# A hybrid decoder block: the short convolution with sequence rows on partitions, its shifted copies made by DMA; first loads and last scalings in another order

## The chip, the core and the metric

The kernel runs on one core of a Trainium2 chip. The core has TensorE (PE, with its weight loads as PEld), VectorE (DVE), ScalarE (ACT), GpSimd (POOL) and SyncE (SP), which work from queues of their own and meet at semaphores, and 16 DMA engines that serve the DMA queues of SyncE and of ScalarE. The metric is the device time of one execution in microseconds (us).

## What is computed

The reference, cut to what matters. All of it is float32; x is 1 x 256 x 2048.

```python
proj = rmsnorm(x, norm_mix) @ w_in          # q, k, v, o, i, f, cb, cc, cx, ga, gb
hm = mlstm_chunkwise(q, k, v, i + b_igate, f + b_fgate)     # 8 heads, chunks of 128
y_a = (sigmoid(o) * rmsnorm_per_head(hm) * mh_norm) @ w_branch_a
p = cc * cx                                  # 256 rows x 2048 channels
u[t] = conv_w[0]*p[t-2] + conv_w[1]*p[t-1] + conv_w[2]*p[t]   # zero ahead of row 0
y_b = (cb * u) @ w_branch_b
x = x + (sigmoid(ga) * y_a + sigmoid(gb) * y_b) @ w_out
x = x + (silu(hf @ w_gate) * (hf @ w_up)) @ w_down          # hf = rmsnorm(x, norm_ffn)
out = rmsnorm(x, norm_final)
```

## The kernel before

**Products.** A float32 product is made of three in `float32r`: the activations and the weights are each split into a rounded part (`_hi`) and a rest (`_lo`), and hi*hi, hi*lo and lo*hi are summed in PSUM. The weights come in chunks of 1 MB (128 partitions x 2048 columns). SyncE loads a chunk into one of four `w_raw` slots, ScalarE rounds it into `w_hi` (`split`, through `copy` at L616), VectorE subtracts into `w_lo` (`split`, L1064), TensorE multiplies: 16 products of 512 columns with `w_hi`, then 8 with `w_lo`. `w_hi` and `w_lo` have two slots. A slot of `w_raw` is free once `w_lo` is made (`lo_split`), one of `w_lo` once TensorE has ended the chunk (`lo_used`). Every engine runs an order written out by hand and waits on counting semaphores.

**Stages.** The head (x and its norm; the chunks of q and k; the gates), three pairs of column blocks for q, k and v, then four turns of the convolution, then six pairs (`p` = FRONT = 3 to 8; o, ga, gb), then the two branches (`G_Y`), the output projection, the feed-forward and the final norm. In pairs, steps named in `FRONT_S` (4 and 6 in pair FRONT) save a product by sums of weights: there VectorE makes sums (`front_sums`, L1165 to L1170), and `t_lo` (L1193).

**A turn of the convolution** (`conv_turn(i)`, a block of 512 channels) has 12 chunks, j = 0 to 11: cb, cc, cx. The results leave with sequence rows on partitions, 2 x 128 rows: ScalarE takes cb into `nat` (j = 3), TensorE transposes it (`turn_block`, j = 5), ScalarE copies it into `cbT`. Later `nat` takes cc (j = 7), and VectorE multiplies it by cx at the turn's end (L1367, `dve_out`). In the next turn TensorE transposes that too (`turn_p`, behind j = 0), and ScalarE copies it (`p_taken`) into `pT`, which has room for zeros ahead of row 0, and scaled by the last tap into `uT`. With channels on partitions a shift in time is a shift of columns, and a tap is one number per partition: VectorE adds the two other taps (`conv_0` at j = 0, `conv_1` at j = 1, four operations of 256 columns each), multiplies by `cbT`, and after ScalarE's `cu_high` makes `cuT_lo` (`conv_low`, j = 2). The turns also carry two heads of the mLSTM each (`head_turn` behind j = 2, `head_scores` behind j = 3, `head_first`, `head_second` behind j = 6 to 9). The last block's taps fall into pair FRONT, in its steps j = 0, 1, 2. Turns 1 to 3 are a hardware loop (`Fori`) on each engine.

**Head.** SyncE issues `norm_mix`, the first quarter of x, three small loads, and then the first chunk in two halves (L437). TensorE warms up on transposes of `ident`, transposes `vec_rows`, then x. ScalarE rounds the first half chunk between two operations of `x_high`.

**Tail.** The last sums come from PSUM in four steps (`take_main`), VectorE and ScalarE scale by the reciprocal norm (`gained`, `scaled`), GpSimd makes the power, SyncE and ScalarE store.

Of the kernel before, what the change touches and what calls it, by code (L numbers as in the profile page):

```python
# [103 lines left out]
def hybrid_block(nc, x, norm_mix, w_in, b_igate, b_fgate, conv_w, mh_norm, w_branch_a, w_branch_b,  # L104
# [51 lines left out]
    with ExitStack() as ctx:  # L156
# [61 lines left out]
        pT = at("pT", [P, KB, SEQ + 32], F32, s + 4096)  # L218
        PAD = 32 - (TAPS - 1)
# [5 lines left out]
        uT = at("uT", [P, KB, SEQ], F32, s)  # L225
        cbT = at("cbT", [P, KB, SEQ], F32, s + 4096)
# [73 lines left out]
        V_MIX, V_MH, V_FN, V_TAP = 0, KC, 2 * KC, 3 * KC  # L300
# [29 lines left out]
        cb_turned, cb_out = sem("cb_turned"), sem("cb_out")  # L330
        p_turned, p_copied, p_read = sem("p_turned"), sem("p_copied"), sem("p_read")
# [76 lines left out]
        def _(sp):  # L408
# [14 lines left out]
            def load_x(g):  # L423
# [21 lines left out]
            sp.dma_start(gate_bias[:, 0:1], b_igate.rearrange("o h -> h o")).then_inc(small_landed[2], 16)  # L445
            sp.dma_start(gate_bias[:, 1:2], b_fgate.rearrange("o h -> h o")).then_inc(small_landed[2], 16)
# [69 lines left out]
        def _(pool):  # L516
# [30 lines left out]
            pool.memset(pT[:, :, PAD:PAD + TAPS - 1], 0.0).then_inc(setup2, 1)  # L547
# [14 lines left out]
            stage(0)  # L562
            with pool.Fori(1, NB) as i:
                stage(i)
# [50 lines left out]
        def _(act):  # L615
# [41 lines left out]

            act.wait_ge(vec_turned, 1)
# [39 lines left out]
            take(c, 0, qk[:, :, 0:COLS])  # L698
            def gate_rows_1():
# [12 lines left out]
            for q in range(BC):  # L712
                c = Chunk(G_QK + BC + q)
                split(c.next())
                if q == 1:
                    act.wait_ge(setup2, 7)
                    gate_rows_1()
# [53 lines left out]
            def p_taken(d):  # L771

                act.wait_ge(p_turned, d + 1)
                if not starts(d):
                    act.wait_ge(cu_lo, d)
                copy(pT[:, :, 32:32 + SEQ], bank_kt(6)).then_inc(p_copied, 1)
                for k in range(KB):
                    last = copy(uT[:, k, :], bank_kt(6)[:, k, :],
                                scale=vecT[:, bass.ds(V_TAP + (TAPS - 1) * KC + k + d * KB, 1)])
                last.then_inc(p_read, 1)  # L780

            def cu_high(d):
                act.wait_ge(u_done, d + 1)
                copy(cuT_hi[:, bass.ds(d * KB, KB), :], uT[:]).then_inc(cu_hi, 1)

            def conv_turn(i):
# [12 lines left out]
                for j in range(3 * BC):  # L799
# [4 lines left out]
                    if j == 0 and not first:  # L804
                        p_taken(i - 1)
                    if j == 2:
                        if not first:
                            cu_high(i - 1)
# [5 lines left out]
                    if j == 3:  # L814
                        if not first:
                            act.wait_ge(p_turned, i)
                        take(c, 0, nat[:])
# [6 lines left out]
                    if j == 5:  # L824
                        act.wait_ge(cb_turned, i + 1)
# [1379 lines left out]
```

## Time and profile before

| | us |
|---|---|
| median of 3 runs (1713.37 to 1714.48) | 1713.92 |
| the profiled execution | 1713.56 |
| its span, first to last instruction | 1711.7 |
| TensorE busy | 1698.0 |
| VectorE busy | 1281.9 |
| ScalarE busy | 888.0 |
| GpSimd busy | 71.3 |

The granted TensorE clock was 0.999 of full speed over the span. The DMA engines moved 331.39 MB, 194 GB/s on the mean. TensorE's products are pipelined: one of 512 columns has a record of 0.39 us, and the next starts 0.23 us after it, so the starts, not the records' lengths, give its pace. The time beside the span (1713.56 against 1711.7) is what lies around the instructions.

### The profile page before, as it was taken

The page shows a single profiled execution, that of the slowest core. Times are in us where ns is not written, and L with a number is a line of the kernel's source. Part 1 is how long each engine was busy: PE and PEld are TensorE (multiplying, and loading weights), DVE is VectorE, ACT ScalarE, POOL GpSimd, SP SyncE. Part 2 cuts the span into 40 slices and gives each one's busy share as a digit, 9 for nine tenths or more (in the row PEclk, how much of TensorE's full clock was granted, in tenths as well). Part 3 has the DMA queues.
Part 4 walks back from the last instruction along what each step waited for, and adds up shares of the span by engine and source line. Part 5 has one row for each costly group of instructions (what it writes and reads, how often), then busy time and mean ns, then how long its engine had stood idle before and what let it go on. Part 6 is the DMA issues. An engine that isn't in the chain of part 4 may idle for free.

```text
span 1711.7 us, 20301 instructions
## 1 busy us (share of the span) xinstructions
PE 1698.0 (99%) x7673; PEld 1407.2 (82%) x7673; DVE 1281.9 (75%) x1108; ACT 888.0 (52%) x780; POOL 71.3 (4%) x65
## 2 busy tenths in 40 slices
PE   9999999999999999999999999999999999999998
PEld 7888888888878888888888888888888888888886
DVE  5888555566579998865554589888888888898987
ACT  6555544454455555553333465555555555665564
POOL 1000010101030000000000000000000000230000
PEclk9999999999999999999999999999999999999999
DMA  8555545554546555555556556665556655556653
GB/s 284 187 196 197 195 158 189 172 162 162 181 158 221 197 201 209 206 187 187 189 192 226 197 167 204 199 200 198 201 199 199 199 197 196 187 194 221 221 193 115
DMA packets 139185, 331.39 MB, mean 194 GB/s; under 512 B 8721, under 2 KB 8817, under 8 KB 138737
## 3 DMA queue, kind: packets, MB, share of 16 engines
q1 hardware_dynamic: 138976, 329.98, 57.2%
q8 instruction: 43, 0.70, 0.2%
q10 hardware_dynamic: 144, 0.52, 0.1%
q14 instruction: 22, 0.17, 0.0%
HBM read 328.38 MB, written 2.10 MB: 193 GB/s over the span
## 4 chain that ended last, share of the span: by engine, by line
PE 97%; DVE 1%; issue 1%; ACT 0%; DMA 0%; SPq 0%; POOLq 0%; DVEq 0%; POOL 0%; ACTq 0%
PE ps L1713 11%; PE ps L1714 11%; PE ps L1722 11%; PE ps L2032 9%; PE ps L2034 9%; PE ps L2038 9%; PE ps L1821 7%; PE ps L1814 7%; PE ps L1815 7%; PE ps L2113 4%; PE ps L2114 4%; PE ps L2118 4%; PE ps L1739 1%; PE ps L1988 1%; DVE w_lo L1064 0%
## 5 line engine op out<-in xcount | busy, mean ns | idle before, releaser
L1064 DVE TENSOR_TENSOR w_lo<-w_raw,w_hi 128x2048 fp32r<-128x2048 f32 x308 | 709.2, 2306 | 136.9 <-ACT w_hi L616 134.5
L616 ACT ACTIVATE w_hi<-w_raw 128x2048 fp32r<-128x2048 f32 (+1 forms) x309 | 588.8, 1909 | 291.2 <-PE ps L1714 102.8
L1713 PE MATMUL ps<-w_hi,xT_hi 128*128 128x512 f32 x448 | 179.6, 401 | 1.7 <-ACT w_hi L616 1.7
L1714 PE MATMUL ps<-w_hi,xT_lo 128*128 128x512 f32 x448 | 174.6, 390 | 0.0
L1814 PE MATMUL ps<-w_hi,xT_hi 128*128 128x512 f32 x426 | 165.9, 389 | 0.9 <-ACT w_hi L616 0.9
L1815 PE MATMUL ps<-w_hi,xT_lo 128*128 128x512 f32 x426 | 165.7, 389 | 0.0
L2032 PE MATMUL ps<-w_hi,fT_hi 128*128 128x512 f32 x396 | 156.2, 395 | 0.0
L2034 PE MATMUL ps<-w_hi,fT_lo 128*128 128x512 f32 x396 | 154.3, 390 | 0.0
L616 ACT ACTIVATE t_hi<-t_raw 128x1536 fp32r<-128x1536 f32 x45 | 66.9, 1486 | 110.3 <-PE ps L2038 87.8
L2038 PE MATMUL ps<-w_lo,fT_hi 128*128 128x512 f32 x396 | 120.1, 389 | 0.0
L1821 PE MATMUL ps<-w_lo,xT_hi 128*128 128x512 f32 x426 | 112.5, 390 | 0.4 <-DVE w_lo L1064 0.4
L1722 PE MATMUL ps<-w_lo,xT_hi 128*128 128x512 f32 x448 | 110.7, 389 | 0.0
L2113 PE MATMUL ps<-w_hi,a_hi 128*128 128x512 f32 x280 | 109.0, 389 | 0.0
L2114 PE MATMUL ps<-w_hi,a_lo 128*128 128x512 f32 x280 | 108.9, 389 | 0.0
L1713 PEld LDWEIGHTS ps<-w_hi,xT_hi 128*128 128x128 f32 x448 | 84.2, 188 | 19.3 <-ACT w_hi L616 1.9
L1722 PEld LDWEIGHTS ps<-w_lo,xT_hi 128*128 128x128 f32 x448 | 84.1, 188 | 17.5
L1714 PEld LDWEIGHTS ps<-w_hi,xT_lo 128*128 128x128 f32 x448 | 84.2, 188 | 16.8
L1814 PEld LDWEIGHTS ps<-w_hi,xT_hi 128*128 128x128 f32 x426 | 80.0, 188 | 17.8 <-issue 1.3
L1821 PEld LDWEIGHTS ps<-w_lo,xT_hi 128*128 128x128 f32 x426 | 79.9, 188 | 17.5 <-DVE w_lo L1064 1.0
L1815 PEld LDWEIGHTS ps<-w_hi,xT_lo 128*128 128x128 f32 x426 | 80.0, 188 | 16.5
L2038 PEld LDWEIGHTS ps<-w_lo,fT_hi 128*128 128x128 f32 x396 | 74.3, 188 | 15.4
L2032 PEld LDWEIGHTS ps<-w_hi,fT_hi 128*128 128x128 f32 x396 | 74.4, 188 | 15.0 <-issue 0.3
(344 smaller groups left out, 2801.9 us busy)
## 6 DMA issues: line engine op xcount, KB each, us to landing
w_raw<-in_w_in SPq DMA_DIRECT2D x127, 1024.0 KB, 5.0
w_raw<-in_w_gate SPq DMA_DIRECT2D x88, 512.0 KB, 3.8
w_raw<-in_w_up SPq DMA_DIRECT2D x88, 512.0 KB, 4.6
w_raw<-in_w_down SPq DMA_DIRECT2D x44, 1024.0 KB, 5.1
w_raw<-in_w_branch_b SPq DMA_DIRECT2D x16, 1024.0 KB, 5.2
w_raw<-in_w_branch_a SPq DMA_DIRECT2D x16, 1024.0 KB, 5.1
w_raw<-in_w_out SPq DMA_DIRECT2D x16, 1024.0 KB, 5.3
xn<-in_x SPq DMA_DIRECT2D x4, 512.0 KB, 8.6
```

Of the source, the lines that this page charges most:

```text
L616: copy = lambda o, i, **kw: nc.scalar.activation(o, i, ACT.Copy, **kw)
L1064: V.tensor_tensor(w_lo[:, chunk.split, :], w_raw[:, chunk.raw, :], w_hi[:, chunk.split, :].bitcast(F32), ALU.subtract).then_inc(lo_split, 1)
L1713: T.matmul(ps[:, banks + r, :], rows(hi, k, r), w, start=(q == 0 and k == 0), stop=False)
L1714: last = T.matmul(ps[:, banks + r, :], rows(lo, k, r), w, start=False, stop=False)
L1722: last = T.matmul(ps[:, banks + r, :], rows(hi, k, r), w, start=False, stop=(q == BC - 1 and k == KB - 1))
L1814: T.matmul(ps[:, banks[name], :], tile(0, t), moving(0, u), start=begins, stop=False)
L1815: last = T.matmul(ps[:, banks[name], :], tile(1, t), moving(0, u), start=False, stop=False)
L1821: last = T.matmul(ps[:, banks[name], :], tile(0, t), moving(1, u), start=False, stop=ends)
L2032: T.matmul(ps[:, banks[name], :], tile_of(0, k, tile), moving(0, u), start=begins(name) and part is own(name)[0], stop=False)
L2034: return T.matmul(ps[:, banks[name], :], tile_of(1, k, tile), moving(0, u), start=False, stop=False)
L2038: return T.matmul(ps[:, banks[name], :], tile_of(0, k, tile), moving(1, u), start=False, stop=final(name) and part is own(name)[-1])
L2113: T.matmul(ps[:, banks[name], :], tile(0, t), moving(0, u), start=start, stop=False)
```

## The change

The convolution's inputs are no longer transposed. The product `nat` keeps its rows on partitions; a shift in time is then a shift of partitions, and is made by DMA: `late1` is `nat` one row later, `late2` two rows later (`shift_rows`, four transfers on ScalarE's queue, j = 0 of the next turn). The taps lie along the columns, so each tap row is loaded into all 128 partitions (`taps`, on SyncE's queue). VectorE multiplies the three by the taps (`taps_times`, j = 1), sums them and multiplies by `cb` into `cu` (`taps_sum`, j = 2; in pair FRONT j = 5). Only `cu` is transposed (behind j = 5; the last block behind the first chunk of `G_Y`), and its parts are made straight from PSUM (`cu_high`, `cu_low`). The turns are written out where they were loops. In the head the small loads leave SyncE's queue, in part for ScalarE's; `conv_w` isn't loaded there; VectorE rounds the first half chunk; the rest of `vec_rows` is transposed after chunk 1 and taken by ScalarE behind chunk 3, and TensorE waits for that before chunk 4. In the tail two operations of `gained` stand earlier.

```diff
@@ SyncE
-            sp.dma_start(vec_rows[V_MH:V_MH + KC, :], kp(mh_norm)).then_inc(small_landed[0], 16)
-            sp.dma_start(vec_rows[V_FN:V_FN + KC, :], kp(norm_ffn)).then_inc(small_landed[0], 16)
-            sp.dma_start(vec_rows[V_TAP:V_TAP + TAPS * KC, :],
-                         conv_w.rearrange("o j (k p) -> (o j k) p", p=P)).then_inc(small_landed[0], 16)
...
-            with sp.Fori(0, NB) as i:
+            for i in range(NB):
                 for n, c in enumerate((C_CB, C_CC, C_CX)):
-                    load_block(G_CONV + n * BC, i, 3 * BC, w_in_k, c + i * COLS)
+                    load_block(G_CONV + (3 * i + n) * BC, 0, 0, w_in_k, c + i * COLS)
+                if i > 0:
+                    sp.wait_ge(u_done, i)
+                for j in range(TAPS):
+                    sp.dma_start(taps[j][:], conv_w[:, j, i * COLS:(i + 1) * COLS].to_broadcast([P, COLS])).then_inc(
+                        taps_landed, 16)
@@ GpSimd
+            pool.wait_ge(act_out, A_CONV)
+            pool.memset(late1[0:1, 0, :], 0.0).then_inc(late_zero, 1)
+            pool.memset(late2[0:2, 0, :], 0.0).then_inc(late_zero, 1)
@@ ScalarE
+            act.dma_start(vec_rows[V_MH:V_MH + KC, :], kp(mh_norm)).then_inc(small_landed[3], 16)
+            act.dma_start(vec_rows[V_FN:V_FN + KC, :], kp(norm_ffn)).then_inc(small_landed[3], 16)
             act.wait_ge(vec_turned, 1)
-            copy(vecT[:], ps[:, 2, 0:96]).then_inc(vec_ready, 1)
+            copy(vecT[:, V_MIX:V_MIX + KC], ps[:, 2, 0:KC]).then_inc(vec_ready, 1)
             act.wait_ge(vec_ready, 1)
             x_high(0, range(2))
-            act.wait_ge(half_landed, 16)
-            copy(w_hi[:, 0, 0:CH // 8], w_raw[:, 0, 0:CH // 8]).then_inc(half_hi, 1)
...
+                if q == 1:
+                    act.dma_start(gate_bias[:, 0:1], b_igate.rearrange("o h -> h o")).then_inc(small_landed[2], 16)
+                    act.dma_start(gate_bias[:, 1:2], b_fgate.rearrange("o h -> h o")).then_inc(small_landed[2], 16)
...
             take(c, 0, qk[:, :, 0:COLS])
+            act.wait_ge(vec_turned, 2)
+            copy(vecT[:, V_MH:V_END], ps[:, 3, V_MH:V_END]).then_inc(vec_ready, 1)
...
+            def shift_rows(d):
+
+                act.wait_ge(dve_out, d + 1)
+                if d > 0:
+                    act.wait_ge(u_done, d)
+                for late, n in ((late1, 1), (late2, 2)):
+                    act.dma_start(late[n:P, :, :], nat[0:P - n, :, :]).then_inc(shifted, 16)
+                    act.dma_start(late[0:n, 1, :], nat[P - n:P, 0, :]).then_inc(shifted, 16)
+
+            def cu_high(d, bank):
+                act.wait_ge(cu_turned, d + 1)
+                copy(cuT_hi[:, d * KB:(d + 1) * KB, :], bank_kt(bank)).then_inc(cu_hi, 1)
@@ VectorE
+            dve.wait_ge(half_landed, 16)
+            V.tensor_copy(w_hi[:, 0, 0:CH // 8], w_raw[:, 0, 0:CH // 8]).then_inc(half_hi, 1)
             x_low(0)
...
+            def taps_times(d):
+
+                wide = lambda t: t[:].rearrange("p (o n) -> p o n", o=1).to_broadcast([P, RT, COLS])
+                if d == 0:
+                    dve.wait_ge(late_zero, 2)
+                dve.wait_ge(taps_landed, 16 * TAPS * (d + 1))
+                dve.wait_ge(shifted, 64 * (d + 1))
+                for part, tap in ((late2, taps[0]), (late1, taps[1]), (nat, taps[2])):
+                    V.tensor_tensor(part[:], part[:], wide(tap), ALU.mult).then_inc(tap_step, 1)
+
+            def taps_sum(d):
+
+                dve.wait_ge(tap_step, d * 5 + 2)
+                V.tensor_tensor(late1[:], late1[:], late2[:], ALU.add).then_inc(tap_step, 1)
+                dve.wait_ge(tap_step, d * 5 + 4)
+                V.tensor_tensor(nat[:], nat[:], late1[:], ALU.add).then_inc(tap_step, 1)
+                dve.wait_ge(tap_step, d * 5 + 5)
+                V.tensor_tensor(cu[:, d], nat[:], cb[:], ALU.mult).then_inc(u_done, 1)
...
                         if not first:
-                            conv_1(i - 1)
+                            taps_times(i - 1)
                     if j == 2 and not first:
-                        conv_low(i - 1)
+                        taps_sum(i - 1)
+                    if j == 5 and not first:
+                        cu_low(i - 1, 6)
...
-                    if p == FRONT and j < 3:
-                        (conv_0, conv_1, conv_low)[j](NB - 1)
+                    if p == FRONT and j in (1, 5):
+                        (taps_times if j == 1 else taps_sum)(NB - 1)
...
             for k, (r, name) in enumerate(MAIN):
+                if k == 3:
+                    dve.wait_ge(y_rstd, 1)
+                    dve.wait_ge(y_sum, MAIN_STEPS + 2)
+                    gained(0, NB // 2)
...
-            dve.wait_ge(y_rstd, 1)
-            dve.wait_ge(y_sum, MAIN_STEPS + 2)
-            gained(0, NB // 2)
+            gained(0, NB // 2 + 1)
             dve.wait_ge(y_squared, 8)
             V.tensor_reduce(sums[:, 1:2], ss_y[:, 1, :], axis=AX.X, op=ALU.add).then_inc(y_total, 1)
-            gained(0, NB // 2 + 1)
@@ TensorE
-            pe.wait_ge(small_landed[0], 64)
-            T.transpose(ps[:, 2, 0:96], vec_rows[:], ident[0:96, 0:96]).then_inc(vec_turned, 1)
+            pe.wait_ge(small_landed[0], 16)
+            T.transpose(ps[:, 2, 0:KC], vec_rows[0:KC, :], ident[0:KC, 0:KC]).then_inc(vec_turned, 1)
...
+                if q == 1:
+                    pe.wait_ge(small_landed[3], 32)
+                    T.transpose(ps[:, 3, 0:V_END], vec_rows[0:V_END, :], ident[0:V_END, 0:V_END]).then_inc(vec_turned, 1)
-            pe.wait_ge(vec_ready, 1)
+            pe.wait_ge(vec_ready, 2)
...
-                    if j == 0 and not first:
-                        turn_p(i - 1)
...
-                    if j == 5:
-                        pe.wait_ge(act_out, A_CONV + 1 + i * 2)
+                    if j == 5 and not first:
+                        pe.wait_ge(u_done, i)
                         pe.wait_ge(scores_done, i * 2 + 2)
-                        turn_block(nat, 6, cb_turned)
+                        turn_block(cu[:, i - 1], 6, cu_turned)
                     if j == 6:
-                        pe.wait_ge(cb_out, i + 1)
+                        if not first:
+                            pe.wait_ge(cu_lo, i)
                         head_first(0)
```

## Rows read from the trace of the kernel before

**Rows 1.** The page, part 1: busy time, share of the span, instructions of each engine.

```profile
PE 1698.0 (99%) x7673; PEld 1407.2 (82%) x7673; DVE 1281.9 (75%) x1108; ACT 888.0 (52%) x780; POOL 71.3 (4%) x65
```

**Rows 2.** The chain that ended last, convolution turns 0 and 1: start, us, what.

```profile
258.13 1.81 PE ps L1722 x8
...
263.57 1.82 PE ps L1722 x8
265.39 0.87 PE ps L1739 x8
...
269.92 1.81 PE ps L1722 x8
...
281.73 1.81 PE ps L1722 x8
```

**Rows 3.** Timeline of TensorE in pair FRONT: start, us, operation, count, idle time before it.

```profile
500.99 2.08 PE L1821 MATMUL ps<-w_lo,xT_hi 128*128 128x512 f32 x8
503.96 0.47 PE L1814 MATMUL ps<-w_hi,xT_hi 128*128 128x512 f32 x1 [0.90 <-ACT w_hi L616]
...
507.75 0.50 PE L1821 MATMUL ps<-w_lo,xT_hi 128*128 128x512 f32 x1 [0.35 <-DVE w_lo L1064]
```

**Rows 4.** Timeline of VectorE in pair FRONT.

```profile
480.44 1.41 DVE L1367 SCALAR_TENSOR_TENSOR nat<-ps,r_x,nat 128x512 f32<-128x512 f32 x2 [2.91 <-PE ps L1722]
...
496.03 1.22 DVE L1165 TENSOR_TENSOR late_t_raw<-w_raw 128x1024 f32<-128x1024 f32 x1
...
501.96 1.75 DVE L1397 TENSOR_TENSOR late_form_lo<-late_form_raw,late_form_hi 128x1536 fp32r<-128x1536 f32 x1
```

**Rows 5.** DMA view, 1700 to 1712: packets, MB, share of 16 engines; issues, KB, landing.

```profile
q10 hardware_dynamic: 144, 0.52, 10.9%
...
out_y<-y ACTq DMA_DIRECT2D x1, 512.0 KB, 3.7
```

**Rows 6.** DMA view of the whole span: packets by size; first and last of the issues.

```profile
DMA packets 139185, 331.39 MB, mean 194 GB/s; under 512 B 8721, under 2 KB 8817, under 8 KB 138737
...
w_raw<-in_w_in SPq DMA_DIRECT2D x127, 1024.0 KB, 5.0
...
gate_bias<-in_b_fgate SPq DMA_DIRECT2D x1, 0.0 KB
```

**Rows 7.** Timeline of VectorE in convolution turn 1.

```profile
259.99 1.41 DVE L1367 SCALAR_TENSOR_TENSOR nat<-ps,r_x,nat 128x512 f32<-128x512 f32 x2 [2.87 <-PE ps L1722]
...
276.36 2.28 DVE L1064 TENSOR_TENSOR w_lo<-w_raw,w_hi 128x2048 fp32r<-128x2048 f32 x1
```

**Rows 8.** DMA view, 250 to 500 us: SyncE's queue.

```profile
q1 hardware_dynamic: 19691, 42.66, 51.1%
```

**Rows 9.** Stretches: us, busy PE, PEld, DVE, ACT, POOL, granted clock, DMA share, GB/s.

```profile
1709.00:1711.70 2.70, 0.00 (x0) 0.00 (x0) 0.00 (x0) 0.00 (x0) 0.00 (x0) 0.50 0.59 234
```

**Rows 10.** Timeline of the head, all engines.

```profile
1.67 3.25 PE L1754 MATMUL ps<-ident 128*128 128x128 f32 x14 [1.67 <-POOL half L523]
...
13.24 8.38 SPq L445 DMA_DIRECT2D gate_bias<-in_b_igate  x1
...
18.72 1.57 ACT L616 ACTIVATE xT_hi<-ps,vecT 128x256 fp32r<-128x256 f32 x4 [2.89 <-PE ps L1739]
```

**Rows 11.** The chain that ended last, head.

```profile
1.65 0.45 SPq L429
...
3.07 5.59 DMA w_raw<-in_w_in
...
9.79 0.50 PE ps L1713
```

**Rows 12.** Timeline, 33 to 36 us: TensorE starts chunk 4, ScalarE takes chunk 3's result.

```profile
34.41 0.39 PE L1713 MATMUL ps<-w_hi,xT_hi 128*128 128x512 f32 x1
...
34.66 1.27 ACT L633 ACTIVATE qk<-ps,r_x 128x512 f32<-128x512 f32 x2 [2.12 <-PE ps L1722]
```

**Rows 13.** Timeline of the tail, GpSimd.

```profile
1705.18 1.00 POOL L611 TENSOR_TENSOR r_x<-sums,half 128x1 f32<-128x1 f32 x1 [2.56 <-DVE sums L1690]
```

More of the change, by code:

```diff
@@ L224, in hybrid_block @@
         s += 4096 + KB * (SEQ + 32) * 4
-        uT = at("uT", [P, KB, SEQ], F32, s)
-        cbT = at("cbT", [P, KB, SEQ], F32, s + 4096)
+        late2 = at("late2", [P, RT, COLS], F32, s)
+        cb = at("cb", [P, RT, COLS], F32, s + 4096)
+        taps = [at(f"tap{j}", [P, COLS], F32, o)
+                for j, o in enumerate((R2 + 12288, R2 + 14336, R2 + AT + 12288))]
+        cu = at("cu", [P, NB, RT, COLS], F32, R2 + AT)
         s += 8192
@@ L768, in _ @@
                         first_out(p, j)
[L771 to L784, printed above, removed]
+            def shift_rows(d):
[8 more added lines that the diff above has]
+                copy(cuT_hi[:, d * KB:(d + 1) * KB, :], bank_kt(bank)).then_inc(cu_hi, 1)
             def conv_turn(i):
@@ L804, in conv_turn @@
                     if j == 0 and not first:
[L805 removed]
+                        shift_rows(i - 1)
                     if j == 2:
                         if not first:
[L808 removed]
                             act.wait_ge(second_done, i * 2)
@@ L815, in conv_turn @@
                         if not first:
-                            act.wait_ge(p_turned, i)
-                        take(c, 0, nat[:])
+                            act.wait_ge(u_done, i)
+                        take(c, 0, cb[:])
                         for b in range(2):
@@ L823, in conv_turn @@
                             last.then_inc(exped, 1)
-                    if j == 5:
-                        act.wait_ge(cb_turned, i + 1)
-                        if not first:
-                            act.wait_ge(u_done, i)
-                        copy(cbT[:], bank_kt(6)).then_inc(cb_out, 1)
+                    if j == 5 and not first:
+                        cu_high(i - 1, 6)
                     if j == 6:
@@ L846, in _ @@
             conv_turn(0)
-            with act.Fori(1, NB) as i:
+            for i in range(1, NB):
                 conv_turn(i)
@@ L859, in _ @@
                     if p == FRONT and j == 0:
-                        p_taken(NB - 1)
+                        shift_rows(NB - 1)
                     if p == FRONT and j == 2:
-                        cu_high(NB - 1)
                         act.wait_ge(late_form_step, 5)
@@ L879, in _ @@
                         front_out(PAIRS - 1, j - 1)
+                    if i == 0 and j == 0:
+                        cu_high(NB - 1, 4)
                     if i == 0 and j < BC:
-                        group_hi(GRP_HM + j + 1, hmT_hi, j * KB, V_MH, 4 + j % 2 * 2)
+                        group_hi(GRP_HM + j + 1, hmT_hi, j * KB, V_MH, 6 - j % 2 * 2)
                     if i > 0 and j == 1:
@@ L1371, in _ @@
             conv_turn(0)
-            with dve.Fori(1, NB) as i:
+            for i in range(1, NB):
                 conv_turn(i)
@@ L1913, in conv_turn @@
                         head_second(1)
-            def turn_p(d):
-                pe.wait_ge(dve_out, d + 1)
-                pe.wait_ge(h1_done, d * 2 + 2)
-                turn_block(nat, 6, p_turned)
             conv_turn(0)
-            with pe.Fori(1, NB) as i:
+            for i in range(1, NB):
                 conv_turn(i)
@@ L1936, in _ @@
                     front_step(p, j)
-                    if p == FRONT and j == 0:
-                        turn_p(NB - 1)
             for i in range(NB):
```

63 lines of the change are left out of this document (26 added, 37 removed).

## The prediction

> **What bounds the kernel now.** I read the page first. TensorE is busy 1698.0 us of a span of 1711.7, VectorE 75%, ScalarE 52% [rows 1]. So time is won only by giving TensorE less to do or by removing its few waits, and anything that makes it wait is paid in full. Then the chain, in one turn of the convolution: a chunk (24 products) takes 5.44 us from one group of eight low products to the next (258.13 to 263.57, and this is across the end of a loop turn, so the loop costs nothing); with the eight transposes of `turn_p` behind it, it takes 6.35 us, so one transposed block costs 0.91 us [rows 2]. VectorE is not the bound there, but its next `w_lo` gates TensorE's low products, and its queue is in order: whatever it waits for, `w_lo` waits for too. The only stage in which TensorE waited in mid-kernel is pair FRONT, right after the convolution [rows 3, 4]. The three other places are the first load, the step at 34.4 us, and the tail.
>
> **Transposes removed.** Eight blocks (four `turn_p`, four of `cb`) become four of `cu`: 4 x 0.91 = 3.64 us off TensorE, with nothing beside them to hide it. ScalarE loses `p_taken` and the `cbT` copy and gains four DMA issues a turn; VectorE gets about two more products of 1.22 us [rows 4] a turn, and neither is full [rows 1]. `cu_high` and `cu_low`, each like one such product, stand between `cu`'s transposes and `head_first`, a chunk (5.4 us) apart, where `cbT` stood: hidden.
>
> **The shifted copies.** This is the term that decides. Each turn copies `nat` twice, by 127 and by 126 rows of 4 KB, and VectorE waits for all four transfers in `taps_times`, with `w_lo` of chunk 3 queued behind. No transfer in the trace has such a row count. The nearest is ScalarE's store of 128 rows of 4 KB: 3.7 us from issue to landing; its 144 packets took 10.9% of 16 engines over 11.7 us, 20.5 us in all, so 0.16 us a row, eight rows (1.3 us) on each engine, and 2.4 us that are fixed [rows 5]. Sixteen engines would take the copies in about 1.3 us each. One engine would take 127 x 0.16 = 20.3 us. Which end is nearer? The 144 packets are 128 rows and 16 closing packets: equal shares, one closing packet per engine. The two `gate_bias` transfers have eight rows. The DMA view of the whole span lists 417 transfers, the first and last of them shown. Of the 8721 packets under 512 B, 2048 are pieces of `wg_raw`, and 6673 are left. 415 transfers at 16 closing packets make 6640, which leaves 33 for the two biases: 16 of data and 16 closing packets, eight each (one is left over). Had they been closed on 16 engines it would be 49 [rows 6]. So the number of engines followed the number of rows, in equal shares. 127 is a prime: its equal share is all of it, on one engine; 126 rows part into 14 shares of nine. I take the one-engine end.
>
> A page of the Trainium skill (DMA: Bandwidth & Descriptors, Why a DMA increments its semaphore by 16 and not by 1) states this rule, the largest count up to 16 that divides the row counts, and names 127 partitions as one engine; the trace agrees as far as its 8 and 128 rows go. By that page's figure of some 27 GiB/s for an engine (Specifications) the copy would take about 18 us and not 20.3, an estimate that would put the whole forecast near 1778 us.
>
> **When the copies land.** In turn 1 the product that fills `nat` ends at 261.40 [rows 7], so the issue is at 261.45. The same engine still has weight chunks to carry: over 250 to 500 us, 40 chunks took 51.1% of 16 engines, 3.2 us of each engine per chunk [rows 8], and two loads become free to start meanwhile (behind `w_lo` 1 and 2). Landing: 261.45 + 2.4 + 20.3 + 1.4 (its nine rows of the second copy) + 6.4 = 291.95. Three products of 128x1024 (1.15 each beyond the first's start; 1.22 by itself, rows 4) are 3.5, `w_lo` 2.3 [rows 7]: chunk 3's low part is there at 297.8. TensorE, 0.91 us ahead without `turn_p`, asks for it at 281.73 - 0.91 = 280.8 [rows 2]. It waits 17.0 us; three turns, 51.0 us. Nothing gives it back: TensorE's work follows the wait, and the other engines are ahead again afterwards.
>
> In pair FRONT the product ends at 481.85, the copies land at 481.90 + 30.5 = 512.4, and `taps_times` 3.5, the sums of chunk 4 2.6 and `w_lo` of chunk 3 2.3 end at 520.8, against 500.99 - 0.91 = 500.1 asked [rows 3, 4]: 20.7 us. Then `late_form_lo`, `late_t_lo` and `w_lo` (5.7 us, by their starts) reach 526.5, where TensorE arrives at 525.8: 0.7 more. Sum 21.4 us.
>
> **The clock.** TensorE's work ends ahead of the tail; in the span's last 2.7 us, with no TensorE instruction, the granted clock is 0.50, which is 1.2 GHz [rows 9]. A wait of 17 us is longer than the whole tail, so TensorE should come back at 1.2 GHz. At the start, 14 transposes took 3.25 us, 232 ns each [rows 10], against 109 ns in a turn [rows 2], though the clock's row reads 1.00 there: about 1.6 us lost. I take 1.6 per wait, four times, 6.4 us, between 0 and 13.
>
> **The stalls that go.** In pair FRONT TensorE was 1.16 us late at 503.96 (due at 500.99 + 1.81 = 502.80) and 0.51 late at 507.75 (due at 507.24, 14 products of 0.227 and 0.1 for the first after a wait) [rows 3]. Both, 1.67, came from `p_taken` and VectorE's queue of taps, and go, whichever way the copies run, since 21.4 is counted from a TensorE that never waits.
>
> **The head.** Three small loads leave SyncE's queue ahead of `w_raw`, so it is issued at 1.65 instead of 3.07 and lands at 8.66 - 1.42 = 7.24 [rows 11]. Its rounding moves to VectorE, which had no such copy: 0.6 to 1.2 us by the 1.22 of a 128x1024 product; I take 1.15. `x_low` now stands behind it, one product of 256 columns, 0.4. TensorE starts at 8.9 instead of 9.79 [rows 11]: 0.85 won (0.3 to 1.4).
>
> **A wait added.** TensorE now waits for `vec_ready` 2 ahead of chunk 4. ScalarE gives it only after `take` of chunk 3: it starts at 34.66 when TensorE has ended, 1.27 for two evictions, some 0.25 for the 32 columns (under the 0.63 of 512). TensorE goes on at about 36.1 instead of 34.41 [rows 12], its first product 0.1 slower: 1.8 lost (1.5 to 2.3). TensorE has nothing else in its queue, so nothing hides it. The new 48-column transpose costs 0.1. The bias loads move to ScalarE's queue in q = 1, where it idled 2.89 us [rows 10]: hidden at 0.4 each.
>
> **The tail.** VectorE's `gained(0, 2)` goes ahead of the last `take_main`, 0.13 us of delay; `gained(0, 3)` no longer runs beside GpSimd's power, which took 1.00 us there [rows 13]; if that beside it cost it two fifths, -0.3 net (-0.5 to +0.2).
>
> **Sum.** -3.64 - 1.67 - 0.85 + 1.8 + 0.1 - 0.3 = -4.6. The copies: 51.0 + 21.4 + 6.4 = 78.8. Together +74.2 on the profiled execution's 1713.56 us (span 1711.7; the median of the three runs is 1713.92, 0.02% away): 1788 us. The tap loads (0.75 MB a turn) and the unrolled loops' instructions lie beside DMA engines that are half idle: nothing, a few tenths at worst.
>
> **Rivals.** First, the copies run on all sixteen engines, in unequal shares (eight rows on most, seven on one). For it: the trace has no prime row count; against it: every count that it has was shared equally. Then both land about 8 us after issue (2.4 + 2.6 + a chunk's 3.2), near the end of VectorE's `w_lo` 2, and `w_lo` 3 is ready 5 us before TensorE asks in a turn and 1.6 us before in pair FRONT; what is left is the -4.6: 1709.0 us, faster by 0.27%. The point that decides is a landing 30.5 - 17.0 = 13.5 us after issue in a turn and 9.8 in pair FRONT; below these nothing is paid. Second, the same, and ScalarE's queue stops at the biases: SyncE stood 8.38 us at `in_b_igate` behind `wg_raw` [rows 10]. If a transfer on ScalarE's queue stood as long, `x_high(2)` would be 8.4 - 2.9 = 5.5 us late and so would TensorE: 1714.5, no change. Against it: that queue has nothing else in it. Third, one engine but quicker: the weight chunks do not add up on it and the clock stays, 4 x 6.4 + 6.4 = 32 us less, 1756; that is the lower end of the forecast's own range. The upper end, with rows at the 48 engine-us per MB of the weights (25 us a copy, +19) and 13 for the clock, is about 1814.
>
> **How the numbers follow.** One engine: 0.81, and its own range 1750 to 1818 holds nearly all of that. Sixteen engines: 0.14; with ScalarE stopped 0.03; others 0.02. The range is 1750 to 1818, so it leaves out the two cases near 1709 and 1714, under 2 in 10. About 0.2% (3.4 us) is what a measurement can tell from no change. Faster by more: 0.13 (the sixteen-engine case, less the part in which its 4.6 us shrink below 3.4). Within: 0.05. Slower: 0.82.
>
> **What would show it.** Right: four gaps on TensorE of 15 to 21 us, each in chunk 3 after a turn's end, released by `w_lo`; VectorE idle ahead of the tap products, released by a DMA of `late`; a landing of 20 to 31 us for the 127 rows; the granted clock falling in each gap; `nat`'s transposes gone (64 to 32 of `cu`). Wrong: a landing under 10 us, then TensorE is busy throughout and the time is near 1709. A gap of 1.8 us at 36 us shows the added wait, `w_raw` rounded at about 7.3 us the head. Wrong in size: a landing of 20 us with the chunks beside it (then about 1760), or ScalarE held at its issues, which would move the gap to an earlier chunk.

## The result and the profile after

The changed kernel takes 1796.28 us (median of four runs, 1796.11 to 1796.54), beside 1713.93 for the kernel before on the same chip: 1.0481 times as long, 95% interval 1.0468 to 1.0494. That is 82.35 us slower; the forecast was 1788, with a range from 1750 to 1818.

The page of the changed kernel, busy time, granted clock in 40 slices, and the chain's shares, to set beside [rows 1]:

```profile
PE 1714.9 (96%) x7642; PEld 1417.4 (79%) x7642; DVE 1292.3 (72%) x1097; ACT 872.9 (49%) x756; POOL 71.7 (4%) x66
...
PEclk9999998989798999999999999999999999999999
...
PE 88%; DMA 4%; ACTq 3%; DVE 2%; issue 1%; ACT 0%; DVEq 0%; POOLq 0%; POOL 0%
```

TensorE has less to do (31 records fewer) and is busy longer, because its granted clock falls in the slices of the convolution. The chain has 4% in DMA and 3% in ScalarE's issues (ACTq). Its waits view (the engine and its line <- whom that waited for; us in total, times, the longest) names the places:

```profile
PE ps L1732 <- DVE w_lo L1068: 27.9, 3, 9.6
...
PE ps L1723 <- ACT w_hi L619: 20.8, 3, 7.3
...
PE ps L1834 <- DVE w_lo L1068: 12.0, 1, 12.0
...
PE ps L1827 <- ACT w_hi L619: 6.7, 1, 6.7
```

Three turns and pair FRONT, two waits in each: about 7 us for `w_hi` ahead of the second chunk behind `nat`, then 9 to 12 us for `w_lo`. The chain that ended last shows both causes in turn 1 (start, us, what):

```profile
263.14 0.74 ACTq L786
...
264.52 11.68 ACTq L786
...
276.24 18.86 DMA late<-nat
...
298.71 2.21 DVE w_lo L1068
...
300.97 3.57 PE ps L1732 x8
```

ScalarE issues the 127-row copy at 263.14. Its third issue, that of the 126 rows, does not come back for 11.68 us, and `w_hi` stands behind it. In the three other places it is already the second issue, that of the single wrapped row, which takes 11.38 to 11.80 us. The copies land at 295.1, 32.0 us after the first issue. VectorE's products and `w_lo` follow, and TensorE's eight low products, which took 1.81 in [rows 2], take 3.57. The DMA views of 283 to 295 us, and then of its last 8 us alone (287 to 295), show who is slow (queue: packets, MB, share of 16 engines; q1 is SyncE's queue, q10 ScalarE's):

```profile
q1 hardware_dynamic: 523, 1.04, 28.0%
q10 hardware_dynamic: 55, 0.20, 4.7%
```
```profile
q10 hardware_dynamic: 37, 0.13, 4.1%
q1 hardware_dynamic: 31, 0.06, 2.0%
```

55 packets of the copies in 12 us took 4.7% of 16 engines, 9.0 us in all, 0.16 us each as in [rows 5]. In the last 8 us both queues together took 6.1% of 16 engines, which is 0.98 of one: one engine's worth of work at a time, and a third of it is SyncE's packets.

### The profile page after: what moved, and what is told of

Same layout as the page of the kernel before. It is cut to its first block, busy times and chain, and to the rows that moved or that the text cites. A ratio compares the mean times of both kernels' runs of the same rounds, so it can differ in the third digit from the quotient of the medians.

```text
span 1794.5 us, 19781 instructions
## 1 busy us (share of the span) xinstructions
PE 1714.9 (96%) x7642; PEld 1417.4 (79%) x7642; DVE 1292.3 (72%) x1097; ACT 872.9 (49%) x756; POOL 71.7 (4%) x66
## 2 busy tenths in 40 slices
DMA packets 142070, 338.77 MB, mean 189 GB/s; under 512 B 9092, under 2 KB 9140, under 8 KB 141616
## 4 chain that ended last, share of the span: by engine, by line
PE 88%; DMA 4%; ACTq 3%; DVE 2%; issue 1%; ACT 0%; DVEq 0%; POOLq 0%; POOL 0%
PE ps L1732 9%; PE ps L1723 9%; PE ps L1724 9%; PE ps L2043 9%; PE ps L2045 8%; PE ps L2049 8%; PE ps L1834 7%; PE ps L1827 7%; PE ps L1828 7%; DMA late<-nat 4%; PE ps L2124 4%; PE ps L2125 4%; PE ps L2129 4%; ACTq L787 2%; ACTq L786 1%
## 5 line engine op out<-in xcount | busy, mean ns | idle before, releaser
L1723 PE MATMUL ps<-w_hi,xT_hi 128*128 128x512 f32 x448 | 183.5, 410 | 22.4 <-ACT w_hi L619 20.8
L1724 PE MATMUL ps<-w_hi,xT_lo 128*128 128x512 f32 x448 | 177.4, 396 | 0.0
L1827 PE MATMUL ps<-w_hi,xT_hi 128*128 128x512 f32 x426 | 167.6, 394 | 6.7 <-ACT w_hi L619 6.7
L1828 PE MATMUL ps<-w_hi,xT_lo 128*128 128x512 f32 x426 | 167.4, 393 | 0.0
L1732 PE MATMUL ps<-w_lo,xT_hi 128*128 128x512 f32 x448 | 115.5, 402 | 27.9 <-DVE w_lo L1068 27.9
L1834 PE MATMUL ps<-w_lo,xT_hi 128*128 128x512 f32 x426 | 114.1, 394 | 12.0 <-DVE w_lo L1068 12.0
L1732 PEld LDWEIGHTS ps<-w_lo,xT_hi 128*128 128x128 f32 x448 | 87.0, 195 | 47.4 <-DVE w_lo L1068 29.1
L1834 PEld LDWEIGHTS ps<-w_lo,xT_hi 128*128 128x128 f32 x426 | 80.9, 190 | 29.3 <-DVE w_lo L1068 12.4
```

The costliest lines, as they stand in the source:

```text
L1723: T.matmul(ps[:, banks + r, :], rows(hi, k, r), w, start=(q == 0 and k == 0), stop=False)
L1724: last = T.matmul(ps[:, banks + r, :], rows(lo, k, r), w, start=False, stop=False)
L1732: last = T.matmul(ps[:, banks + r, :], rows(hi, k, r), w, start=False, stop=(q == BC - 1 and k == KB - 1))
L1827: T.matmul(ps[:, banks[name], :], tile(0, t), moving(0, u), start=begins, stop=False)
L1828: last = T.matmul(ps[:, banks[name], :], tile(1, t), moving(0, u), start=False, stop=False)
L1834: last = T.matmul(ps[:, banks[name], :], tile(0, t), moving(1, u), start=False, stop=ends)
```

## Experiments

**The count of engines (e_split).** Each long copy in two, with row counts that part evenly.

```diff
-                    act.dma_start(late[n:P, :, :], nat[0:P - n, :, :]).then_inc(shifted, 16)
+                    for a, b in ((0, 112), (112, P - n)):
+                        act.dma_start(late[n + a:n + b, :, :], nat[a:b, :, :]).then_inc(shifted, 16)
```

> The changed kernel, but each long copy goes as two transfers with row counts that share out: 127 rows as 112 and 15, 126 rows as 112 and 14. The bytes, the rows' targets and the wait of VectorE stay, six transfers a turn instead of four. Theory (the 127-row transfer is carried by one DMA engine, and its landing is the whole loss): the copies land under 10 us after their issue, no gap stays on TensorE after the turns' ends, TensorE stays at 2.4 GHz throughout the convolution, and the time is 1711 us, 1706 to 1714 (the parts other than the copies, as measured in the changed kernel: chunk 4 starts 2.44 later, 3.64 of transposes and 1.67 of stalls go, the tail 0.14 longer: -2.7 on 1713.9). Rival A (moving rows by one or two partitions, or the 12 MB of extra traffic beside the weights, is slow with any row count): landing stays at 20 us or more and the time above 1760. Rival B (ScalarE's held issue, not the landing, is half of the loss): with six issues a turn ScalarE is held as long as before, a gap of some 7 us stays ahead of the high products of chunk 2, and the time is about 1740.

Measured: 1712.73 us, 0.9994 of before (0.9985 to 1.0003). Same bytes, same shift of partitions: 83.6 us less than the changed kernel, so both rivals fall. VectorE in turn 1 (behind turn 0's `nat`) and in pair FRONT, and TensorE in pair FRONT:

```profile
274.20 2.36 DVE L1277 TENSOR_TENSOR late<-late,tap 128x1024 f32<-128x1024 f32 x2 [2.08 <-DMA late<-nat]
...
491.31 2.36 DVE L1277 TENSOR_TENSOR late<-late,tap 128x1024 f32<-128x1024 f32 x2 [2.19 <-DMA late<-nat]
...
499.64 2.12 PE L1835 MATMUL ps<-w_lo,xT_hi 128*128 128x512 f32 x8 [0.96 <-DVE w_lo L1069]
```

The first issues were at 262.62 and 480.22, so the copies land after 11.5 and 11.0 us, not under 10: six issues take 4.6 us. In a turn that is inside the 13.5 us that the prediction's first rival allowed; in pair FRONT it is 1.2 over its 9.8, and TensorE waits 0.96 and then 0.36 us. These 1.3 us are the larger part of the 1.7 between the expected 1711 and the measured 1712.7.

The pages also allow a count of the engines, by their small packets. Changed kernel, e_split, and e_shares (the next experiment):

```profile
DMA packets 142070, 338.77 MB, mean 189 GB/s; under 512 B 9092, under 2 KB 9140, under 8 KB 141616
```
```profile
DMA packets 142254, 338.77 MB, mean 198 GB/s; under 512 B 9276, under 2 KB 9324, under 8 KB 141800
```
```profile
DMA packets 142115, 338.77 MB, mean 194 GB/s; under 512 B 9137, under 2 KB 9185, under 8 KB 141661
```

If each engine of a transfer adds one closing packet under 512 B, as the prediction read it from [rows 5, 6], cut copies on 16, 15, 16 and 14 engines close 61 times, and uncut ones on 1 and 14 close 15 times: 46 more in each of four places, 184 in all, and 9276 - 9092 is 184. In e_shares 2 + 9, 4 + 11 and 15 + 7 stand for one each in turn: 10 + 14 + 21 = 45, and 9137 - 9092 is 45.

**Two, four and fifteen engines (e_shares).** Only the 127-row copy is cut, another way after each turn.

```diff
+                cut = (118, 116, 120, None)[d]
...
+                    if n == 1 and cut:
+                        act.dma_start(late[n:n + cut, :, :], nat[0:cut, :, :]).then_inc(shifted, 16)
+                        act.dma_start(late[n + cut:P, :, :], nat[cut:P - n, :, :]).then_inc(shifted, 16)
```

> The changed kernel, but the 127 rows of the first copy are cut differently after each turn: after turn 0 as 118 and 9 rows, after turn 1 as 116 and 11, after turn 2 as 120 and 7, and after turn 3 (pair FRONT) left whole. Theory (the number of engines is the largest divisor of the row count up to 16): 118 rows go on 2 engines, 59 each, 9.4 us of transfer; 116 on 4 engines, 29 each, 4.6 us; 120 on 15 engines, 8 each, 1.3 us; 127 on one, 20.3 us. The landing after the first issue is about 20, 15 and 8 us in the three turns, TensorE waits some 4 to 8 us after turn 0, about nothing after turns 1 and 2, and the gap in pair FRONT is that of the changed kernel (6.7 and 12.0 us). Time about 1740, 1730 to 1750. Rival (an engine limit that is all or nothing: any count that is not a multiple of 16 falls on one engine, or the slow copy is due to the shift by one partition): all of 118, 116 and 120 land at 27 us or more and the time is above 1780.

Measured: 1745.88 us (one run). VectorE's first tap product in the four places:

```profile
284.58 2.36 DVE L1281 TENSOR_TENSOR late<-late,tap 128x1024 f32<-128x1024 f32 x2 [12.59 <-DMA late<-nat]
...
360.20 2.36 DVE L1281 TENSOR_TENSOR late<-late,tap 128x1024 f32<-128x1024 f32 x2 [3.86 <-DMA late<-nat]
...
430.97 2.37 DVE L1281 TENSOR_TENSOR late<-late,tap 128x1024 f32<-128x1024 f32 x2 [1.72 <-DMA late<-nat]
...
524.25 2.36 DVE L1281 TENSOR_TENSOR late<-late,tap 128x1024 f32<-128x1024 f32 x2 [13.60 <-DMA late<-nat]
```

From the first issue (263.10, 345.30, 419.53, 492.07) that is 21.5, 14.9, 11.4 and 32.2 us for 2, 4, 15 and 1 engines; 20, 15 and 8 were expected; the 8 had left out that the five issues stand one behind the other (4.5 us there). TensorE waits 7.9 and 1.3 us, then nothing. The more engines the 127 rows are given, the earlier they land. A page of the Trainium skill (DMA: Bandwidth & Descriptors, Why a DMA increments its semaphore by 16 and not by 1) gives the largest divisor up to 16 as the count; the packets and the landings here agree with it for 112 to 127 rows on ScalarE's queue.

**Another queue (e_pool).** In the three turns the same uncut transfers from GpSimd.

```diff
+                    nc.gpsimd.dma_start(late[n:P, :, :], nat[0:P - n, :, :]).then_inc(moved, 16)
+                    nc.gpsimd.dma_start(late[0:n, 1, :], nat[P - n:P, 0, :]).then_inc(moved, 16)
```

> The changed kernel, with nothing cut: in the three turns the same four transfers (127, 1, 126 and 2 rows) are issued from GpSimd's queue instead of ScalarE's, behind GpSimd's work for the heads, with a semaphore of their own; in pair FRONT they stay on ScalarE's queue. Theory (one DMA engine carries 127 rows whichever queue issues them): the copies land 29 to 32 us after their issue in the three turns. ScalarE is no longer held, so the 7 us gap ahead of chunk 2 goes and that in chunk 3 is 16 to 18 us: the time within 5 us of the changed kernel, 1791 to 1799. Rival (GpSimd's queue shares its rows out another way than ScalarE's, eight at most to an engine): the copies land 11 to 14 us after issue, the gaps in the three turns go, those in pair FRONT stay; 3 x 20.4 less, 1735, 1732 to 1740. This rival is what a page of the Trainium skill states (DMA: Bandwidth & Descriptors, Why a DMA increments its semaphore by 16 and not by 1): on trn2 the software queue gives some direct copies all sixteen engines, and names 127 partitions among them.

Measured: 1734.27 us, 1.0118 of before (1.0101 to 1.0135): the rival, to within a microsecond. My theory, that the queue does not matter, falls. GpSimd's issue and VectorE's product:

```profile
262.94 0.79 POOL L573 DMA_DIRECT2D late<-nat  x1 [7.76 <-DVE nat L1382]
```
```profile
271.65 2.36 DVE L1284 TENSOR_TENSOR late<-late,tap 128x1024 f32<-128x1024 f32 x2 [1.99 <-DMA late<-nat]
```

The DMA view gives 4.5 us from issue to landing for the 127 rows, and all four are there 8.7 us after the first issue. So 127 rows are slow on ScalarE's queue, not slow as such. The same section of the Trainium skill (DMA: Bandwidth & Descriptors, Why a DMA increments its semaphore by 16 and not by 1) makes an exception for GpSimd's software queue on trn2, which spreads 127 partitions of some direct copies over all sixteen engines; the trace agrees with it by the 4.5 us. The two gaps in pair FRONT (7.2 and 12.5 us) stay.

**The order of the transfers (e_last).** The 126 rows and the wrapped rows first, the 127 rows last.

> The changed kernel, with the order of the four transfers turned round: the copy by two rows (126 rows) and both wrapped rows first, the 127-row copy last. Nothing else changes. Theory (VectorE's wait for the landing is what TensorE pays, ScalarE's held issue only shifts part of it one chunk forward): ScalarE is not held for 11.7 us by an issue any more, the gap of 7 us ahead of chunk 2's high products vanishes, the gap in chunk 3 grows from 9.3 to about 16, and the time stays within 3 us of the changed kernel: 1796, 1791 to 1799. Rival (the held issue delays more than the landing does): the gap of 7 us goes and none takes its place, so the time falls by 20 to 28 us, to about 1770.

Measured: 1795.33 us, 1.0474 of before (1.0458 to 1.0490). Four issues take 0.6 to 1.0 us each, the gap for `w_hi` is gone, and the one for `w_lo` is 18 us:

```profile
PE ps L1733 <- DVE w_lo L1069: 54.9, 3, 18.5
...
PE ps L1835 <- DVE w_lo L1069: 21.6, 1, 21.6
```

In the changed kernel the same 18 us are made of 7.0 and 9.2 us of waiting and, between them, 2.0 us by which the sixteen high products behind the first wait are slower (5.67 us by their starts instead of 3.63). The held issue moved the first 7 us a chunk forward and cost next to nothing of its own (0.95 us by the medians); the landing is what TensorE pays. It fits that an issue is held when it has rows for the engine on which 127 are queued: with these last, nothing is behind them. That is not shown: in e_shares no issue was held after 59 rows on each of two engines (0.9 us at most), but one took 2.58 us after 29 on each of four.

**A slow copy with cover (e_cover).** e_last, and in pair FRONT VectorE waits behind chunk 6, not 1.

```diff
-                    if p == FRONT and j in (1, 5):
-                        (taps_times if j == 1 else taps_sum)(NB - 1)
+                    if p == FRONT and j == 6:
+                        taps_times(NB - 1)
+                        taps_sum(NB - 1)
```

> e_last (nothing cut: the 126-row copy first, the 127-row copy last, on one engine), and in pair FRONT alone the tap products and sums of VectorE behind chunk 6 instead of behind chunks 1 and 5. In the three turns nothing changes. Theory (what TensorE pays is the place of VectorE's wait, not the copy's length): the copies still land 33 us after nat is filled, TensorE's gap of 21.6 us in pair FRONT goes; seven products and sums of 1.22 us in one place delay one w_lo by up to 4 us. Time 17 to 21 us under e_last: 1776, 1773 to 1779; the three gaps of 18 us in the turns stay. Rival (the slow copy holds back the weights' loads on its engine, so TensorE would wait for w_raw without VectorE's wait too): a wait for w_raw's landing takes the gap's place, and the time falls by less than 10 us.

Measured: 1791.80 us (one run), 3.5 under e_last. The theory failed; of the rival the small gain came, but not its wait for `w_raw`: TensorE waited 15.45 us for VectorE to empty the sums of the pair (`c_o`). The copies did not land 33 us after `nat` was filled (542.41 + 1.41 = 543.8) but 45.5:

```profile
589.38 2.36 DVE L1277 TENSOR_TENSOR late<-late,tap 128x1024 f32<-128x1024 f32 x2 [12.53 <-DMA late<-nat]
...
599.98 0.80 PE L1829 MATMUL ps<-w_hi,xT_hi 128*128 128x512 f32 x1 [15.45 <-DVE c_o L1231]
```

The DMA views from about the issue to the landing, of e_last (541 to 574) and of e_cover (543.5 to 589.3), show what was different:

```profile
q1 hardware_dynamic: 595, 2.24, 20.1%
q10 hardware_dynamic: 304, 1.04, 9.0%
```
```profile
q1 hardware_dynamic: 1926, 7.38, 45.2%
q10 hardware_dynamic: 304, 1.04, 6.7%
```

While VectorE waits, no slot of `w_raw` comes free and the weights stop; with cover they go on: 5.1 MB more, 4.9 chunks, at the 3.2 us per engine of [rows 8] 15.7 us of the one engine's time, against 13.7 that the landing is later (45.5 less e_last's 31.8). So it fits that the long transfer shares its engine with the weights, and that cover lengthens it by theirs; the view of 287 to 295 us in the changed kernel showed both queues on one engine's time.

**The clock (e_fill).** 72 transposes into a free bank inside the wait of the fourth chunk.

> The changed kernel, with 72 transposes of the identity (0.11 us each, 8 us in all, into a free bank that nobody reads) between the high and the low products of the fourth chunk of turns 1 to 3, where TensorE waits 9.3 us. They add no wait and end about 1 us before the wait does, so they cost nothing by themselves. Theory (TensorE comes back from each wait at 1.2 GHz and loses about 1.6 us before it is at 2.4 again): the granted clock stays at 1.00 over the gap and the first low products behind it, 1.6 us less in each of three turns, the time 4.8 us under the changed kernel: 1791.5, 1789 to 1794. Rival (the clock after a wait costs nothing that counts, since VectorE's next chunk is late anyway): the time stays at 1796, within 1.5 us.

Measured: 1790.45 us, 1.0449 of before (1.0433 to 1.0465). Stretches of TensorE behind the gap's start, changed kernel and then e_fill (us, busy and count, granted clock, DMA share, GB/s):

```profile
291.00:301.00 10.00, 0.78 (x5) 0.65 0.02 9
301.00:303.00 2.00, 2.00 (x5) 0.50 0.47 106
303.00:305.00 2.00, 2.00 (x10) 0.71 0.99 318
```
```profile
291.00:300.00 9.00, 8.74 (x77) 1.00 0.02 6
300.00:303.00 3.00, 3.00 (x17) 1.00 0.70 196
303.00:305.00 2.00, 2.00 (x10) 1.00 0.62 229
```

Idle, TensorE falls from 2.4 to 1.2 GHz (0.50) and works at that for some 3 us; kept busy it stays at 1.00. The medians differ by 5.8 us, but not all of it is the clock of these waits. From VectorE's product for `nat` at turn 0's end to that at turn 3's end e_fill takes 273.92 us and the changed kernel 278.88: 4.96 less in three turns (1.57, 0.80 and 2.59), 1.7 a wait. The rest lies ahead of them, where nothing was changed: turn 0's product is 1.18 us earlier already, and e_fill's profiled execution began its first products at 9.02 us and not 9.83, behind quicker warm-ups (see the head below).

**The added wait (e_early).** On e_split, the 32 columns for `vec_ready` 2 are copied at q = 3, ahead of the evictions.

> e_split, with ScalarE's copy of the other 32 columns of the vectors (the one that gives vec_ready 2) ahead of its work for the fourth chunk instead of behind the two evictions of that chunk. Nothing else changes. Theory (TensorE's wait of 1.50 us for ScalarE's vecT at 36.8 us in the changed kernel is a wait that nothing hides): the wait goes, chunk 4 starts 1.65 us earlier, the time is 1.65 us under e_split: 1711.1, 1710.2 to 1711.9. Rival (the wait was cover for the weights: chunk 4's high part or its DMA would have been late anyway): another wait of 0.5 to 1.5 us takes its place in the trace and the time stays at 1712.5.

Measured: 1710.95 us, 0.9986 of before (0.9977 to 0.9995), 1.78 under e_split; 1.5 if each is set against the kernel before on its own chip (1713.48 and 1713.24). Chunk 4 in the changed kernel and in e_early:

```profile
36.85 0.50 PE L1723 MATMUL ps<-w_hi,xT_hi 128*128 128x512 f32 x1 [1.50 <-ACT vecT L619]
```
```profile
34.11 0.39 PE L1724 MATMUL ps<-w_hi,xT_hi 128*128 128x512 f32 x1
```

**The head (e_oldhead, e_bestold).** e_oldhead is e_split with the old order of the first loads; e_bestold is e_best (described next) with the same old order and twelve warm-ups.

> e_split, with the head as in the kernel before (all small vectors loaded on SyncE's queue ahead of the weights, one transpose and one copy for all of them, the first half chunk rounded by ScalarE), without the conv_w rows; so vec_ready 2 is not waited for either. Against e_early it differs in the new head alone. Theory (the new head lets TensorE start up to 0.85 us earlier, but only where its twelve warm-up transposes run at the fast pace; in the profiled runs so far the first product began at 9.02 and 9.28 us after fast warm-ups and at 9.67, 9.83 and 10.08 after slow ones): the first product at 9.6 to 9.9, the time 0.1 to 0.7 us over e_early: about 1711.5. Rival (the new head costs, as the changed kernel's profile said, 0.78 us at chunk 3): 0.5 to 0.8 us under e_early, about 1710.4.

> e_best with the head of e_oldhead: three small vectors on SyncE's queue ahead of the weights, one transpose and one copy, ScalarE rounds the first half chunk, twelve warm-ups. Theory (e_oldhead against e_early, 1710.38 to 1710.95, and its first product at 8.43 against 9.12: with the conv_w rows gone from SyncE's queue the old order of the first loads is the better one, since the first half chunk is rounded at 7.3 instead of 7.8 to 8.2): the first product at 8.4 to 9.0, 0.5 us under e_best: 1707.8, 1707.2 to 1708.4. Rival (the first landings scatter by as much from run to run, and the head's order is worth nothing that counts): within 0.3 of e_best's 1708.3, the first product at 9.0 or later.

Measured: 1710.38 and 1708.48 us, against 1710.95 (e_early) and 1708.27 (e_best): 0.57 less with the old head and 0.21 more, both inside the scatter of either kernel's runs (0.3 to 2.2 us). The old head starts its products at 8.43 and 8.58 and loses the lead while it waits for the next quarter of x (0.23 us and 0.90 us on TensorE) and for `w_hi` (0.19 and 0.28). At chunk 3's low products e_oldhead is 0.15 us ahead of e_early (32.15 and 32.30), and e_bestold 0.48 behind e_best (33.04 and 32.56). The head's order shows nothing in the time; which is better stays open.

**FRONT and the warm-ups (e_best), the tail (e_tail).** e_early with `warm(7)` for `warm(12)` and the tap products of pair FRONT at j = 4; e_tail is that with the old order of the last scalings.

> e_early with two more edits: seven warm-up transposes instead of twelve ahead of the first product, and in pair FRONT the three tap products of VectorE behind chunk 4 instead of behind chunk 1, so that w_lo of chunk 3 is ahead of them. Theory (warm-ups at the slow pace, 231 ns each, bind the start in some runs; in FRONT TensorE was 0.96 and 0.36 us late for w_lo behind the products): the first product at 9.0 to 9.3 us, no wait of TensorE in pair FRONT, 0.5 and 1.4 us less than e_early: 1709.2, 1708.2 to 1710.0. Rival for the start (with fewer warm-ups the products themselves run at the slow pace): first products of 0.78 us each and no gain. Rival for FRONT (VectorE's queue is full behind chunk 4 too): a new wait for w_lo or late_t_lo of about 1 us behind 510 us, and no gain.

> e_best, with the order of the last scalings as in the kernel before: both products gained(0, ..) behind the last take_main, the second one beside GpSimd's power. Theory (the changed order takes the power from 1.00 to 0.56 us and sends the last store 0.44 us earlier after the last product, 4.38 instead of 4.82, but the stores then land later, 4.7 instead of 4.1 us after the last issue): the tail after TensorE's last product begins is 8.95 instead of 9.1 us in the trace, the time 0.1 to 0.2 us under e_best. Rival (the order is worth what the power gains): the tail is 0.3 to 0.4 us longer and the time as much over e_best.

Measured: e_best 1708.27 us (1708.12 to 1708.44), 0.9968 of before (0.9956 to 0.9980), the fastest kernel here: 5.0 us under the one before, TensorE without a wait in pair FRONT. Of its 2.7 us against e_early FRONT's two waits were 1.6; the two edits were not parted, and of the warm-ups I can say only that seven did not bring the start forward (9.38 us, and in e_tail 9.15 with a first product of 0.77 us, which is what the rival for the start had). e_tail took 1708.61; its trace has 9.21 us from the start of the last products to the end, against 9.14. GpSimd's power in e_tail and in e_best:

```profile
1700.02 1.00 POOL L614 TENSOR_TENSOR r_x<-sums,half 128x1 f32<-128x1 f32 x1 [2.60 <-DVE sums L1700]
```
```profile
1699.49 0.56 POOL L614 TENSOR_TENSOR r_x<-sums,half 128x1 f32<-128x1 f32 x1 [2.58 <-DVE sums L1702]
```

The new order wins 0.44 us there, and ScalarE's store lands 4.1 instead of 3.8 us after its issue. By the medians e_tail is 0.34 slower, which is the rival's number, but only 0.07 of it lies in the traces' tails; the last products themselves begin 0.53 us later, where the kernels are the same. Whether the order is worth anything stays open.

## Why the prediction held, and where it missed

Against its own execution (spans 1711.7 and 1794.5) the change cost 82.8 us; the sum said 74.2. By its steps:

- **One engine for 127 rows**: right, shown by e_split, e_shares and the closing packets. The first rival's points of decision, 13.5 and 9.8 us, held in e_split. Its time, 1709.0, did not come of the even shares alone: e_split took 1712.7, 1.3 of the difference being FRONT's two waits and most of the rest head, transpose and tail (below). That e_best's 1708.3 lies near 1709.0 says nothing, since the added wait, which the rival's sum has in it, is gone there.
- **The landing**: 30.5 forecast, 32.0 measured. The shorter transfer that the prediction also weighed, 18 us instead of 20.3, would have put it at 28.2, further off. From landing to TensorE 5.85 forecast, 5.88 measured. TensorE's low products of chunk 3 begin 39.3 us after `nat`'s product against 21.7 before: +17.5 (and the same in turns 2 and 3), where 17.0 - 0.91 = 16.1 were put.
- **The form of the gap**: missed. I had it as one wait in chunk 3, and named ScalarE held at its issues only as a thing that would move it. It was held 11.7 us and the gap came in two, 7.0 and 9.2, with 2.0 us of slow products between; e_last shows that this changed 1 us at most in the sum.
- **The clock**: 1.6 a wait forecast (14 transposes at 232 instead of 109 ns, the rows that it named, give 1.7). Behind chunk 3's wait the three turns lose 1.70, 1.35 and 2.86 us against before, 1.97 on the mean; e_fill took 1.7 of it away. Why the third loses more stays open.
- **A turn**: from turn 0's end to turn 3's end VectorE's product for `nat` moves by 60.14 - 1.71 us (540.58 and 261.70, against [rows 4, 7]), 19.5 for each of the three turns between; the steps give 17.0 + 1.6 - 0.91 = 17.7. The 1.8 that were missed are 1.4 of landing and 0.4 of clock, three times 1.8 is 5.4 us. Most of the whole miss of 8.6 is here.
- **Pair FRONT**: 21.6 net (behind it TensorE's low products begin 81.76 us late, 615.94 against 534.18) against 21.4 + 1.6 - 1.67 - 0.91 = 20.4. The landing took 31.6 us there.
- **Transposes**: right. Turn 0, which has no copy to wait for, gave back 0.91 (chunk 4's low products begin 2.62 late, `nat`'s product 1.71); in e_split, which never waits in a turn, the three others came too (`nat`'s product at turn 3's end 1.66 us ahead of before).
- **The added wait**: 1.8 forecast; chunks 3 and 4's low products begin 7.28 us apart instead of 5.44, 1.84 more, and e_early gave back 1.5 to 1.8.
- **The head**: wrong. 0.85 us won was the forecast; chunk 3's low products began at 33.37 instead of 32.59, 0.78 lost. The first half chunk was rounded at 7.90, in 0.69 instead of 1.15 us, but TensorE's twelve warm-ups, 1.47 us in the trace of before and no term of the sum, ran 2.77 and ended behind it, at 9.83. Among the profiled runs with this head and twelve warm-ups the products began at 9.02, 9.12 and 9.28 us behind quick warm-ups (1.47 us) and at 9.67 to 10.08 behind slow ones (2.17 to 2.77), 8.9 being the forecast; so the step has a scatter of 1 us that one trace of before could not show. The new 48-column transpose cost 0.4, not 0.1: chunks 1 and 2's low products begin 6.75 apart instead of 6.34.
- **The tail**: -0.3 forecast, +0.14 in the trace, and within 0.1 of nothing by e_tail's trace.

Three turns missed by 5.4, pair FRONT by 1.2, head, transpose and tail by 2.0 together, and the chunks behind FRONT by nothing. The sum held because its main term was right in mechanism and nearly in size. It did not need misses that cancel: they all lie on the same side. A trace of before could carry the landing's mechanism because it had a store with 128 rows and two loads with 8; it could not tell how the first 10 us scatter.

## What to carry to other kernels

Ahead of a shift by partitions through DMA, look at the row count, not at the bytes: 127 rows of 4 KB, at 0.16 us each on one engine, are 20 us, and four such copies made this kernel 4.8% longer; a cut at 112, the same bytes in two transfers, took that away, and so did GpSimd's queue where it was tried. Keep what is urgent from standing behind such an issue on its queue, and do not count on cover alone: the copy landed later beside the stream that was to hide it (45.5 us instead of 31.8). And where TensorE waits for a small copy, put that copy ahead of the work that the copying engine does anyway, not behind it (1.5 to 1.8 us here).

## What the runs showed that I had not expected

- In each of four places one issue on ScalarE's queue, behind that of the 127 rows, took 11.38 to 11.80 us (the others 0.6 to 1.6); ScalarE did nothing else in that time. With the 127 rows issued last, none took more than 0.96.
- GpSimd's queue spread the same 127 rows (4.5 us to landing), ScalarE's did not: there they landed with the rest after 32 us.
- A one-engine transfer landed after 32 us with the weights held, and after 45.5 us with 4.9 more chunks beside it.
- In the first 10 us, with the clock's row at 1.00 throughout, the same eight transposes of x, begun between 5.56 and 6.01 us by kernels with the same head, took 1.1 us in some executions and 1.97 in others.
